# The last 16 up chunks of a transformer kernel by Strassen's method, with their weight sums made by adding DMAs from GpSimd's queue

## The chip, the core and the metric

One core of one Trainium2 chip. Engines: TensorE (PE), VectorE (DVE), ScalarE (ACT), GpSimd (POOL), SyncE (SP), 16 DMA engines. The metric is the device time of one execution in microseconds (us); the kernel before takes 1288.5 us in the median of three runs (1288.05 to 1291.14).

## The reference

Two transformer blocks over 512 tokens of 1024 features, all float32. The last part is the one that matters here:

```
def conv_ffn(xn, w_up, conv_w, conv_b, w_down):
    h = xn @ w_up                       # 1024 -> 2 x 2816
    a, b = jnp.split(h, 2, axis=-1)
    c = causal depthwise convolution of a, 3 taps, + conv_b
    return (jax.nn.gelu(c, approximate=False) * b) @ w_down

def second_block(...):
    z = rmsnorm(h, mix_norm_g) @ w_in
    ... pool, rwkv and differential attention mixers ...
    h = h + y @ w_out
    h = h + memory_cross_attention(...)
    h = h + conv_ffn(rmsnorm(h, ffn_norm_g), w_up, conv_w, conv_b, w_down)
```

The first block (two kinds of attention, gates, output projections) and the mixers of the second take the first 926 us of the span.

## The kernel before

**Arithmetic.** Every float32 factor is split into a high half (ACT copies it to the type float32r) and a low half (raw minus high, on DVE or POOL). A product is three matmuls: high x high, high x low, low x high (`mm3`, L488 is the matmul itself). Activations are laid out as [128 features, tokens], so the weights are the stationary operand and the tokens the moving one.

**The stream of weights.** SP loads 85 chunks of 1 MB (8 k x 256 columns for 128 partitions) into a ring of three raw slots (L2615; L2569 for the first 15). ACT makes the high half of a chunk (L1192) in a ring of two, as soon as the chunk before the last is used up; POOL makes the low half in four parts of 512 columns (`low_weights`, L2499), and PE waits part by part. Each engine works through its instructions in the order written; there is no planner.

**Up stage.** For each j of 11, two chunks (half a, half b), each with two tiles of 128 features: 4 x 8 x 3 = 96 matmuls of 512 columns. The four results go to banks 0 to 3 in turn. DVE moves an `a` tile out of its bank times the inverse norm (L2411), does the three taps (L2413 to L2415), ACT does the gelu (L1818), DVE multiplies with the norm and with the `b` tile in its bank (L2433, L2435). The forms for the down stage are made tile by tile (L2421, L2424, L2425, high half L1211, low half L1855).

**Down stage.** It already works by Strassen's method in the Winograd form: 2x2 quarters of the weights and of the activations, seven products with 4 pieces of weights each, DOWN = 28 pieces, each 11 k x 3 matmuls of 256 columns (the token half). A piece has its own bank; DVE adds it to `xres` (L2441), and some products start on the bank of an earlier one once that has been moved. Pieces are loaded by SP (L2631, 704 KB), high half on ACT (L1202), low half on DVE (L1855) or, for the first four and each fourth, on POOL (L2557).

**Sums of the down weights.** Four of the seven products need sums of quarters of the weights (S1 to S4). They are made in DRAM (`sums_kept`) in the first 460 us: ACT issues plain copies of a quarter (S1 and S3 from A21 at L1367, S2 from S1 at L1392, S4 from S2 at L1496), and POOL adds another quarter by adding DMAs, four per sum (`add`, L2509), which stand in its queue between the low halves of chunks 15 and 16, 17 and 18, 22 and 23, 34 and 35. POOL waits for the copy before it issues the adds.

## Time and profile before

| | |
|---|---|
| median of 3 runs | 1288.5 us |
| profiled execution | 1291.47 us, its span 1289.7 us |
| mean granted TensorE clock | 0.997 |
| PE / DVE / ACT / POOL busy | 97 / 54 / 44 / 41% |
| up stage, first matmul to first matmul of down | 926.27 to 1174.53 us |
| down stage, to its last matmul | 1286.51 us |

The span is the time from the first to the last instruction in the profile; the execution's own time is a little longer. A busy share is the time in which an engine had at least one instruction in work. Matmuls overlap: one of 512 columns is recorded with some 396 ns, but they start every 234 ns, so the pace is read from starts, not from lengths.

### The profile page before, as it was taken

The numbers are of one execution on the slowest core, as the hardware profiler recorded it, in microseconds if no ns is written. First come the engines' busy times: TensorE is split into PE (matmuls) and PEld (weight loads), VectorE is DVE, ScalarE is ACT, GpSimd is POOL, SyncE is SP. The second block draws the span as 40 slices with busy tenths as digits, with TensorE's granted clock in tenths as the row PEclk, the third lists the DMA queues.
The fourth block names the chain that finished last, engine by engine and source line by source line (L and its number), as shares of the span: only waits on it lengthen the run. The fifth ranks groups of instructions, "written<-read, shape, count | busy, mean of one in ns | idle before, by whom it ended". The sixth has DMA issues, their size and how long they took to land.

```text
span 1289.7 us, 20794 instructions
## 1 busy us (share of the span) xinstructions
PE 1253.3 (97%) x8570; PEld 1019.5 (79%) x8570; DVE 699.2 (54%) x1093; ACT 568.5 (44%) x870; POOL 530.7 (41%) x424
## 2 busy tenths in 40 slices
PE   6999999999999999999998899999999999999999
PEld 5788888866678888767786767788788888888999
DVE  3250004886431266686557657265565665766773
ACT  6541444786665233354544544353422221224452
POOL 6544454322234544534242126331444444546321
PEclk9999999999999999999999999999999999999999
DMA  9836795612115452412220013310222222224554
GB/s 387 348 131 243 248 230 191 163 50 97 51 66 188 122 163 79 181 66 76 69 107 16 3 66 131 135 61 34 99 98 98 81 87 94 99 88 172 166 185 151
DMA packets 24907, 165.05 MB, mean 128 GB/s; under 512 B 2792, under 2 KB 2920, under 8 KB 11504
## 3 DMA queue, kind: packets, MB, share of 16 engines
q1 hardware_dynamic: 20448, 128.15, 27.9%
q10 hardware_dynamic: 2064, 24.07, 5.0%
q0 software_dynamic: 2304, 11.54, 4.5%
q8 instruction: 68, 1.11, 0.3%
q14 instruction: 23, 0.19, 0.0%
HBM read 157.43 MB, written 29.38 MB: 145 GB/s over the span
## 4 chain that ended last, share of the span: by engine, by line
PE 89%; DVE 4%; ACT 3%; POOL 2%; issue 1%; DMA 0%; SPq 0%; DVEq 0%; ACTq 0%
PE banks L488 87%; PE banks L495 2%; DVE arena L1985 1%; POOL h_low L2557 1%; DVE arena L1982 1%; DVE arena L1987 1%; POOL weights_low L2557 1%; DMA arena<-in_mem 0%; ACT weights_high L1192 0%; ACT arena L1238 0%; ACT memory_high L1248 0%; ACT arena L1416 0%; ACT arena L1417 0%; ACT arena L1415 0%; DVE arena L1943 0%
## 5 line engine op out<-in xcount | busy, mean ns | idle before, releaser
L2499 POOL TENSOR_TENSOR weights_low<-weights,weights_high 128x512 fp32r<-128x512 f32 x324 | 433.2, 1367 | 580.5 <-ACT weights_high L1192 580.5
L488 PE MATMUL banks<-h_high_low,weights_high 128*128 128x512 f32 x880 | 358.2, 407 | 1.6 <-ACT arena L1443 1.6
L488 PE MATMUL banks<-h_low,weights_high 128*128 128x512 f32 x880 | 348.9, 397 | 0.0
L488 PE MATMUL banks<-h_high_low,weights_low 128*128 128x512 f32 x880 | 348.8, 396 | 0.0
L1192 ACT ACTIVATE weights_high<-weights 128x2048 fp32r<-128x2048 f32 (+2 forms) x90 | 156.3, 1737 | 243.1 <-PE banks L488 226.0
L488 PEld LDWEIGHTS banks<-h_high_low,weights_high 128*128 128x128 f32 x880 | 166.0, 189 | 46.0 <-issue 5.8
L488 PEld LDWEIGHTS banks<-h_low,weights_high 128*128 128x128 f32 x880 | 166.0, 189 | 41.8 <-issue 3.6
L488 PEld LDWEIGHTS banks<-h_high_low,weights_low 128*128 128x128 f32 x880 | 165.8, 188 | 40.4
L488 PE MATMUL banks<-arena 64*64 64x64 f32 (+6 forms) x1800 | 118.1, 263 | 4.1 <-issue 2.6
L488 PEld LDWEIGHTS banks<-arena 64*64 64x64 f32 (+3 forms) x1800 | 85.9, 148 | 29.9 <-issue 23.2
L1238 ACT ACTIVATE arena<-banks 128x256 f32<-128x256 f32 (+4 forms) x82 | 41.9, 519 | 53.4 <-PE banks L495 35.1
L2411 DVE TENSOR_TENSOR arena<-banks,sums 128x512 f32<-128x512 f32 x22 | 15.2, 692 | 78.1 <-PE banks L488 73.0
L488 PE MATMUL banks<-t_high,weights_low 128*128 128x256 f32 x198 | 55.6, 281 | 0.0
L488 PE MATMUL banks<-weights_high,h_high_low 128*128 128x256 f32 (+1 forms) x192 | 55.3, 288 | 0.3 <-ACT arena L1238 0.3
L488 PE MATMUL banks<-weights_high,h_low 128*128 128x256 f32 (+1 forms) x192 | 54.2, 282 | 0.0
L488 PE MATMUL banks<-weights_low,h_high_low 128*128 128x256 f32 (+1 forms) x192 | 54.1, 282 | 0.0
L1221 ACT ACTIVATE sums<-xres 128x512 f32<-128x512 f32 x32 | 20.2, 631 | 70.3 <-DVE xres L2065 39.3
L1938 DVE COPY arena<-banks 128x256 f32<-128x256 f32 (+3 forms) x40 | 25.3, 632 | 47.1 <-PE banks L488 46.2
L488 PE MATMUL banks<-t_high,weights_high 128*128 128x256 f32 x154 | 43.5, 283 | 2.5 <-issue 1.5
L488 PE MATMUL banks<-t_high,h_high_low 128*128 128x256 f32 x154 | 42.7, 277 | 0.0
L2557 POOL TENSOR_TENSOR weights_low<-weights,weights_high 128x384 fp32r<-128x384 f32 (+1 forms) x20 | 21.3, 1094 | 47.3 <-ACT weights_high L1202 47.3
L495 PE MATMUL banks<-consts,arena 128*128 128x128 f32 x245 | 37.2, 277 | 1.6 <-DVE arena L2222 0.8
(360 smaller groups left out, 2371.9 us busy)
## 6 DMA issues: line engine op xcount, KB each, us to landing
weights<-in_stream SPq DMA_DIRECT2D x82, 1024.0 KB, 4.8
sums_kept<-in_down POOLq DMA_DIRECT2D x16, 704.0 KB, 12.8
arena<-in_ada SPq DMA_DIRECT2D x8, 1024.0 KB, 11.9
weights<-in_down SPq DMA_DIRECT2D x9, 704.0 KB, 4.1
weights<-sums_kept SPq DMA_DIRECT2D x9, 704.0 KB, 4.0
sums_kept<-in_down ACTq DMA_DIRECT2D x2, 2816.0 KB, 21.4
sums_kept<-sums_kept ACTq DMA_DIRECT2D x2, 2816.0 KB, 12.6
h<-sums_kept SPq DMA_DIRECT2D x7, 704.0 KB, 4.2
```

What stands on the lines that cost most here:

```text
L488: ins = nc.tensor.matmul(o, lhsT, rhs, start=start, stop=stop, skip_group_check=skip)
L495: ins = nc.tensor.transpose(o, i, ident[0:rows, 0:rows])
L1192: nc.scalar.activation(hi_of(c)[:, cols], raw_of(c)[:, cols], ACT.Copy)\
L1221: nc.scalar.activation(SQ[n][i % 2][:, 0:width], src[:, k, 0:width], ACT.Square)\
L1238: nc.scalar.activation(dst, s_, ACT.Copy).then_inc(ring_.out(key), 1)
L1938: nc.vector.tensor_copy(dst, o if src is None else src(o)).then_inc(ring_.out(key), 1)
L1982: link(stt(w, o[:, :, 0:end], 0.0, w, ALU.max, ALU.add))
L1985: ins = nc.vector.tensor_tensor_scan(v, ones(end), v, 0.0, ALU.mult, ALU.add)
L1987: tt(w, o[:, :, 0:end], w, ALU.subtract).then_inc(M2.out(("a", i)), 1)
L2411: tt(a[:, 2:T + 2], o, rms[:, :], ALU.mult).then_inc(M.out(("up", m, 0)), 1)
L2499: nc.gpsimd.tensor_tensor(lo_of(c)[:, cols], raw_of(c)[:, cols], hi_of(c)[:, cols].bitcast(F32), ALU.subtract).then_inc(sem("weights_split ...
L2557: nc.gpsimd.tensor_tensor(down_lo(i)[:, cols], down_raw(i)[:, cols], down_hi(i)[:, cols].bitcast(F32), ALU.subtract).then_inc(sem("down_lo ...
```

## The change

- The up stage does only 3 of its 11 j in the old way (`UP_PLAIN`), six chunks, with banks 0 to 5 in turn. `STREAM` is 69 in place of 85.
- The other 16 tiles of `a` and 16 of `b` are 16 Strassen chunks (`UP`). Each is a 2x2 scheme: the 1024 inputs (k) in two halves, two tiles of 128 outputs, the 512 tokens in two halves; even chunks are two tiles of `a`, odd chunks the two tiles of `b` beside them. A chunk has seven products (P1, R5, P3, P6, R7, Q4, P2) of 4 k x 3 matmuls of 256 columns. The order is in `UP_STEPS`: in step i products P1 and R5 of chunk i, Q4 and P3 of chunk i-1, R7, P6 and P2 of chunk i; the last chunk has another order. In a chunk P6 adds onto the bank of P1, Q4 onto R7's, P3 onto R5's, each after what is there has been copied or moved.
- Weights come as 112 pieces of 256 KB, two by two (pairs): six raw slots, four high slots, cut out of the old rings. ACT makes the high half of a pair (1024 columns), DVE the low half, for 2 of 7 pairs POOL (2 x 512 columns).
- ACT copies P1 and P6 (`keep`), DVE makes the four quarters of a chunk in five moves (`up_out`), ACT does the first tap and its bias (`tap`), DVE the other two. The norm is multiplied into the tokens beforehand (`h_raw`), so the moves of the Strassen chunks have no multiplication by it. The token sums (4) and seven low and high halves are made during the plain chunks.
- The forms of the down stage are made in another order, mostly at the start of the product before; only each fourth piece's low half is on POOL.
- All sums of weights, for down and now for up (`up_sums`, 4 sums of 4 MB), are made from POOL's queue: 8 plain copies and 32 adding DMAs. ACT issues none. SP waits for all of them before the first up piece.

The core of the diff:

```diff
-STREAM = 85
+UP_PLAIN = 3
+UP = 2 * (KF // 2 - UP_PLAIN)
+STREAM = 63 + 2 * UP_PLAIN
+KH, TH = KD // 2, T // 2
+UP_STEPS = [[(c, f) for c, fs in ((i, (P1, R5)), (i - 1, (Q4, P3)), (i, (R7, P6, P2))) if 0 <= c < UP for f in fs]
+            for i in range(UP + 1)]
+UP_STEPS[UP - 1] = [(c, f) for c, fs in ((UP - 1, (P1, R5, R7, P6)), (UP - 2, (Q4, P3)), (UP - 1, (P2,))) for f in fs]
+PAIR_RAW, PAIR_HI = 6, 4
+PAIRS_POOL = [q for q in range(UP_PAIRS) if q % 7 in (2, 5)]
...
-        FROM_POOL = tuple(i for i in range(DOWN) if i < DOWN_PAIRS or i % DOWN_PAIRS == 0)
+        DOWN_FREE = [104, 108, UP_N, UP_N, UP_N]
+        FROM_POOL = tuple(i for i in range(DOWN) if i % DOWN_PAIRS == 0)
... PE
-            for j in range(KF // 2):
+            M.use([0, 1, 2, 3, 4, 5])
+            for j in range(UP_PLAIN):
...
+            for n, (c, f) in enumerate(UP_SEQ):
+                if f == P6:
+                    pe.wait_ge(sem("up_copied"), 2 * c + 1)
+                elif f == Q4:
+                    pe.wait_ge(sem("product_moved"), moved_at(c, SUM3))
+                elif f == P3:
+                    pe.wait_ge(sem("product_moved"), moved_at(c, C22))
+                elif c < 2:
+                    M.take(pe, ("up", c, f, "bank"))
+                elif f == P1:
+                    pe.wait_ge(sem("up_copied"), 2 * (c - 2) + 2)
+                else:
+                    pe.wait_ge(sem("product_moved"), moved_at(c - 2, {R5: C12, R7: C21, P2: C11}[f]))
+                q = n // 2
+                if q in PAIRS_POOL:
+                    pe.wait_ge(sem("piece_low_pool"), 2 * PAIRS_POOL.index(q) + n % 2 + 1)
+                elif n % 2 == 0:
+                    pe.wait_ge(sem("piece_low"), PAIRS_DVE.index(q) + 1)
+                if c == 0:
+                    pe.wait_ge(sem("token_split"), T_ORDER.index(f) + 1)
+                for k in range(KH):
+                    mm(o, whi[:, k, :], right[0], k == 0 and f not in (P6, Q4, P3), False, skip=True)
+                    mm(o, whi[:, k, :], right[1], False, False, skip=True)
+                    mm(o, wlo[:, k, :], right[0], False, last, sem("product_done") if last else None, skip=True)
... ACT
-            for to in (S1, S3):
-                act.dma_start(sums_kept[to], down_in[A21]).then_inc(sem("sums_copied"), 16)
+            for i, step in enumerate(UP_STEPS):
+                for c, f in step:
+                    if n and UP_SEQ[n - 1][1] in (P1, P6):
+                        keep(*UP_SEQ[n - 1])
+                    if n % 2 == 0:
+                        pair_high(n // 2 + 3)
+                    ... taps, gelus, first high halves
... DVE
+                if f == P2:
+                    moved_(tt(to_tile(c, 0, 0), up_bank(c, P2), k1, ALU.add))
+                    dve.wait_ge(sem("up_copied"), 2 * c + 2)
+                    moved_(tt(k3, up_bank(c, R7), k2, ALU.subtract))
+                    dve.wait_ge(sem("product_moved"), moved_at(c, SUM3))
+                    moved_(tt(to_tile(c, 1, 1), k3, up_bank(c, R5), ALU.subtract))
+                elif f == Q4:
+                    moved_(tt(to_tile(c, 1, 0), up_bank(c, Q4), k2, ALU.subtract))
+                else:
+                    moved_(tt(to_tile(c, 0, 1), up_bank(c, P3), k2, ALU.add))
+            for i, step in enumerate(UP_STEPS):
+                for c, f in step:
+                    if n:
+                        up_out(n - 1)
+                    if n % 2 == 1:
+                        low_pair((n + 5) // 2)
+                    if i % 2 == 1:
+                        ... first_form at R5, conv of one tile at P6
+                    elif i:
+                        if f == (R5 if i < UP else Q4):
+                            conv(up_tile(i - 2, 1), False)
+                        if f == P6:
+                            gact_out(i - 1)
... POOL
+            low_weights(0, 12)
+            copy(sums_kept[S1], down_in[A21])
+            copy(sums_kept[S3], down_in[A21])
+            low_weights(12, 15)
+            add_down(S1, A22, 2)
+            add_down(S3, A11, 2)
+            low_weights(15, 18)
+            copy(sums_kept[S2], sums_kept[S1], 2)
+            copy(up_sums[S1], up_in[A21])
+            low_weights(18, 20)
+            copy(up_sums[S3], up_in[A21])
+            low_weights(20, 22)
+            add_down(S2, A11, 5)
+            add_up(S1, A22, 5)
+            low_weights(22, 24)
+            add_up(S3, A11, 5)
+            low_weights(24, 26)
+            copy(sums_kept[S4], sums_kept[S2], 5)
+            copy(up_sums[S2], up_sums[S1], 5)
+            low_weights(26, 28)
+            add_down(S4, A12, 7)
+            add_up(S2, A11, 7)
+            low_weights(28, 33)
+            copy(up_sums[S4], up_sums[S2], 7)
+            low_weights(33, 36)
+            add_up(S4, A12, 8)
... SP
+            sp.wait_ge(sem("sums_added"), 8 * 16 * DOWN_PAIRS)
+            for n, (c, f) in enumerate(UP_SEQ):
+                    if q < PAIR_RAW:
+                        sp.wait_ge(used[last % RAW], last // RAW + 1)
+                    else:
+                        sp.wait_ge(sem("product_done"), 2 * (q - PAIR_RAW) + 2)
+                sp.dma_start(piece_of(pair_raw, n), up_from[f][c]).then_inc(pair_loaded(q)[0], 16)
```

The third argument of `copy` is the number of sums (four adds each) that must have landed, that of `add_down` and `add_up` the number of copies.

## Rows read from the trace of the kernel before

**Rows 1.** the page, parts 1 and 2: TensorE, its clock in 40 slices

```profile
PE 1253.3 (97%) x8570; PEld 1019.5 (79%) x8570; DVE 699.2 (54%) x1093; ACT 568.5 (44%) x870; POOL 530.7 (41%) x424
...
PEclk9999999999999999999999999999999999999999
```

**Rows 2.** chain of waits in order of time: start us, us, what

```profile
878.97 295.74 PE banks L488 x1274
...
1184.26 12.15 POOL h_low L2557 x8
```

**Rows 3.** timeline of PE (start us, us, engine, line, op): stage starts, last matmul

```profile
926.27 0.39 PE L488 MATMUL banks<-h_high_low,weights_high 128*128 128x512 f32 x1
...
1174.53 0.28 PE L488 MATMUL banks<-t_high,weights_high 128*128 128x256 f32 x1
...
1286.51 0.28 PE L488 MATMUL banks<-t_high,weights_low 128*128 128x256 f32 x1
```

**Rows 4.** timeline of POOL in the up stage, chunks two apart

```profile
951.89 5.05 POOL L2499 TENSOR_TENSOR weights_low<-weights,weights_high 128x512 fp32r<-128x512 f32 x4 [4.84 <-ACT weights_high L1192]
...
974.39 5.03 POOL L2499 TENSOR_TENSOR weights_low<-weights,weights_high 128x512 fp32r<-128x512 f32 x4 [5.39 <-ACT weights_high L1192]
```

**Rows 5.** timeline of DVE: its first move of the up stage, its last moves

```profile
935.40 0.69 DVE L2411 TENSOR_TENSOR arena<-banks,sums 128x512 f32<-128x512 f32 x1 [5.11 <-POOL arena L2550]
...
1279.04 0.42 DVE L2441 TENSOR_TENSOR xres<-xres,banks 128x256 f32<-128x256 f32 x1 [3.25 <-PE banks L488]
...
1286.82 0.42 DVE L2441 TENSOR_TENSOR xres<-xres,banks 128x256 f32<-128x256 f32 x1 [3.47 <-PE banks L488]
```

**Rows 6.** timeline of weight loads (PEld) at the start of the down stage

```profile
1191.74 0.19 PEld L488 LDWEIGHTS banks<-t_high,weights_high 128*128 128x128 f32 x1 [1.66 <-issue]
...
1195.04 0.19 PEld L488 LDWEIGHTS banks<-t_high,weights_high 128*128 128x128 f32 x1 [1.10 <-POOL h_low L2557]
```

**Rows 7.** groups by form, 870 to 1170 us: shapes, count, busy us, mean ns

```profile
L2499 POOL TENSOR_TENSOR weights_low<-weights,weights_high 128x512 fp32r<-128x512 f32 x96 | 130.5, 1389 | 165.1 <-ACT weights_high L1192 165.1
...
L2415 DVE SCALAR_TENSOR_TENSOR arena<-arena,params 128x512 f32<-128x512 f32 x22 | 26.3, 1194 | 0.8
...
L2421 DVE TENSOR_TENSOR arena<-arena 128x256 f32<-128x256 f32 x11 | 16.6, 1512 | 0.0
...
L1192 ACT ACTIVATE weights_high<-weights 128x2048 fp32r<-128x2048 f32 x24 | 46.0, 1915 | 155.3 <-PE banks L488 155.3
...
L1818 ACT ACTIVATE arena<-arena 128x512 f32<-128x512 f32 x22 | 13.6, 624 | 9.0 <-DVE arena L2415 9.0
```

**Rows 8.** three lines by themselves: ns of one, min/median/max, first and last start

```profile
L2415 DVE SCALAR_TENSOR_TENSOR arena<-arena,params x22: 752/754/1823, 937.5 to 1165.7; 128x512 f32<-128x512 f32 x22
...
L2425 DVE SCALAR_TENSOR_TENSOR arena<-arena x11: 411/420/1512, 1081.7 to 1178.6; 128x256 f32<-128x256 f32 x11
...
L1855 DVE TENSOR_TENSOR weights_low<-weights,h_high_low x8: 1619/1626/2170, 1189.2 to 1273.8; 128x1408 fp32r<-128x1408 f32 x8
```

**Rows 9.** DMA view, issues: count, KB each, median us to landing

```profile
sums_kept<-in_down POOLq DMA_DIRECT2D x16, 704.0 KB, 12.8
...
weights<-in_down SPq DMA_DIRECT2D x9, 704.0 KB, 4.1
...
sums_kept<-sums_kept ACTq DMA_DIRECT2D x2, 2816.0 KB, 12.6
...
out<-xres SPq DMA_DIRECT2D x8, 256.0 KB, 2.7
```

**Rows 10.** timeline of POOL: four adding DMAs, low halves of chunk 18

```profile
156.52 3.49 POOL L2509 DMA_DIRECT2D sums_kept<-in_down  x4
...
181.56 5.04 POOL L2499 TENSOR_TENSOR weights_low<-weights,weights_high 128x512 fp32r<-128x512 f32 x4 [1.36 <-ACT weights_high L1192]
```

**Rows 11.** line L2615 by itself: its 69 loads, us to landing

```profile
DMA to landing us min/median/max: 4.6/4.8/17.4
```

**Rows 12.** timeline of ACT: the chunk load that it waits for

```profile
149.08 1.91 ACT L1192 ACTIVATE weights_high<-weights 128x2048 fp32r<-128x2048 f32 x1 [5.82 <-DMA weights<-in_stream]
```

More of the change, by code:

```diff
@@ L443, in down_loaded @@
             if s < RAW:
-                return loaded[s], 16 * ((STREAM + i % DOWN_RAW - 2) // RAW + 1 + turn)
+                return loaded[s], 16 * (sum(c % RAW == s for c in range(2, STREAM)) + turn + 1)
             return sem(f"first{s - RAW}_loaded"), 16 * (turn + 2)
@@ L1819, in _, with gelu, first_high_of @@
-            assert chunks[0] == STREAM + HI
-            for i in range(HI, DOWN):
+            def gelu(m):
+                act.wait_ge(sem("conv"), m + 1)
+                nc.scalar.activation(gact_raw[:, m, :], gact_raw[:, m, :], ACT.Gelu).then_inc(sem("gelu"), 1)
+            def first_high_of(m):
+                if m < DOWN_K:
+                    if m < 2 * UP_PLAIN:
+                        M.wait_out(act, ("up", m, 1))
+                    else:
+                        act.wait_ge(sem("forms_made"), made_at("gact", m))
+                    high(t_hi[0][:, m, :], q11[:, m, :], sem("forms_hi"))
@@ new lines, in _ @@
+            split_weights()
+            for m in range(2):
+                gelu(m)
+            split_weights()
+            for i, f in enumerate(T_ORDER):
+                act.wait_ge(sem("token_made"), KD + 4)
+                high(th_hi[f], th_raw[f], sem("token_hi"))
+            split_weights()
+            for m in range(2):
+                first_high_of(m)
+            for m in range(2, 4):
+                gelu(m)
+            split_weights()
+            for m in range(2, 4):
+                first_high_of(m)
@@ new lines, in _, with form_high @@
+            for _ in range(HI):
+                split_weights()
+            assert chunks[0] == STREAM + HI
+            def form_high(f):
+                act.wait_ge(sem("product_done"), UP_N + DOWN_PAIRS * (f - 1))
+                for g, (first, last) in enumerate(GROUPS):
+                    act.wait_ge(sem("forms_made"), {R5: made_at("T1", DOWN_K - 1), P6: made_at("T2", g), R7: made_at("T3", g),
+                                                    Q4: made_at("T4", g)}.get(f, made_at("gact", KF - 1)))
+                    high(t_hi[f % 2][:, first:last, :], form_raw[f][:, first:last, :], sem("forms_hi"))
@@ L1821, in _ @@
+            down_high(1)
+            form_high(R5)
+            for i in range(2, DOWN):
                 down_high(i)
@@ new lines, in gact_out @@
+            def gact_out(c):
+                for half in range(2):
+                    m = up_tile(c, half)
+                    dve.wait_ge(sem("gelu"), m + 1)
+                    if half == 0:
+                        dve.wait_ge(sem("product_moved"), moved_at(c, C12))
+                    tt(gact_raw[:, m, :], gact_raw[:, m, :], other[:, half, :], ALU.mult).then_inc(sem("forms_made"), 1)
+                    if m >= DOWN_K:
+                        first_form(m)
+            for m in range(2):
+                conv(m, True)
@@ new lines, in add_up @@
+            def add_up(to, what, copied):
+                pool.wait_ge(sem("sums_copied"), 16 * copied)
+                for p in range(DOWN_PAIRS):
+                    chunks = slice(UP // 4 * p, UP // 4 * (p + 1))
+                    pool.dma_start(up_sums[to, chunks], up_in[what, chunks], accum_op=ALU.add, max_dma_last_dim=8192)\
+                        .then_inc(sem("sums_added"), 16)
+            low_weights(0, 12)
+            copy(sums_kept[S1], down_in[A21])
+            copy(sums_kept[S3], down_in[A21])
```

422 lines of the change are left out of this document (282 added, 140 removed).

## The prediction

> **What bounds the kernel now.** I read the page first: PE is busy for 97% of the span, and the granted clock is in the top tenth in all 40 slices [rows 1], so TensorE runs at its 2.4 GHz level and the clock is no term. The chain of waits in order of time says the same for the part that changes: from 878.97 us on it is matmuls, except for a hop over ACT and POOL up to 1196 [rows 2]. A busy PE can still wait inside, so next come single matmuls. The up stage starts at 926.27, the down stage at 1174.53, the last matmul at 1286.51 [rows 3]. In the up stage POOL's work on one weight chunk (48 matmuls of 512 columns) recurs every 22.50 / 2 = 11.25 us [rows 4], so 22 chunks take 247.5 of the 248.26 us between the two starts; the rest (0.8 us) is the norm's matmul. The up stage has no waits: it is bound by matmuls alone. In the down stage the last products end 3.89 us apart (7.78 / 2) for 33 matmuls of 256 columns [rows 5], 0.1179 us each; 28 products need 108.9 us and take 112.1, so 3.2 us are waits, 2.8 of them seen as two idle gaps of weight loads at 1191.7 and 1195.0 [rows 6], where POOL's and DVE's low halves came late.
>
> **The matmuls.** Of 22 plain chunks 6 stay; 16 go: 16 x 11.25 = 180.0 us out. In comes Strassen's method: 16 chunks x 7 products x 4 k x 3 = 1344 matmuls of 256 columns. The up stage of before has none of these, but the down stage has the same form (fp32r parts, 128x128 weights, 256 columns) at 0.1179 us: 158.5 us in. Net -21.5 us. The ends of that price: half of a 512-column matmul (0.2344 / 2 = 0.1172) gives 157.5, and 0.12 gives 161.3; it is a small uncertainty. The shorter products (12 matmuls against 33) bring a wait every 1.41 us, but in the down stage products with a wait at each k run at the same pace.
> The Trainium skill, page "TensorE: Matmul & The Clock Gate", section "Back-to-back issue gap", speaks against the change: it gives a sustained 131 ns at 512 columns and 81 ns at 128; read linearly (an estimate from that page, 98 ns at 256), 768 large ones would be 101 us, 1344 small ones 132 us, and the change would cost 31 us. The trace decides otherwise: 234 and 118 ns, a ratio of 1.99.
>
> **DVE in the Strassen part**, by two chunks (14 products, 168 matmuls, 19.8 us). An op with two SBUF inputs and 256 columns takes 0.41 to 0.42 alone, one of 1408 takes 1.62 [rows 8], so 1.04 ns a column, and 1024 columns 1.22. Five of the seven weight pairs get their low half here: 6.1. Ten moves of products: 4.2. Four taps of the convolution at 0.75 (752 to 754 ns undisturbed [rows 8]; L2415's mean of 1194 has POOL beside it [rows 7]): 3.0. Two products with the gelu at 0.69: 1.4. Forms for the down stage: 0.8 to 1.7. Sum 15.5 to 16.4. While POOL subtracts, DVE's two-input ops stretch: L2421 takes 1.51 where 0.42 is its length alone, and so loses 1.1; L2415 loses 0.44 on average [rows 7, 8]. Over the 96 POOL ops of that stretch these two groups alone lose 11 x 1.1 + 22 x 0.44 = 21.8, so a POOL op costs DVE at least 0.23 and at most 1.1; I take 0.6. There are 4 POOL ops in 19.8 us, so +2.4 (0.9 to 4.4). DVE needs 18 to 19 of 19.8 us: under PE, but near.
> ACT: seven high halves of 1024 columns (between 0.62 at 512 and 1.92 at 2048 [rows 7]: 1.05) 7.4, two taps, two gelus, four copies of products and up to two forms at 0.62 at most: 6.2; 13.6 of 19.8. POOL 4 x 1.39 = 5.6.
> The order matters as much as the sums. The tightest handover is product Q4 of the chunk before: it adds onto the bank of R7, and waits for DVE's SUM3, which waits for P2. Two products of the next chunk lie between (P1, R5: 2.8 us); DVE needs 2 moves, 0.84. So it may come 2 us late to P2. From P3 to P2 it has 4.2 us and, in even steps, one move, two low halves at most, the gelu products and forms, some 4.5 to 5.3: it is late by 0.3 to 1.1 there, and is not seen by PE. A low half is ordered five products (7.1 us) ahead of its use. I put 1.5 us on this (0 to 8, below).
>
> **The start of it.** DVE begins at 935.40 [rows 5]; the plain chunks end at 926.27 + 0.8 + 67.5 = 994.6. In between, DVE does 6 convolutions (2.84 each, 17.0), 8 scalings of the tokens (6.0), 4 sums (4.9), 7 low halves of the sums (8.5), 5 gelu products (6.9), 4 forms (1.7) and 2 low pairs (2.4): 47.4 of 59.2 us, with 16 POOL ops at 0.6 another 9.6, and 2.3 us of waiting for the second product: 59.3. The last piece is fixed: product (5, up) is full at 983.3, after it DVE has 2.84 + 0.8 + 2.4 + 1.4 = 7.5 us, to 990.8, if it is punctual, and the bank of tile 4 is wanted at 994.6. Six banks for the plain chunks keep the sums of tokens between a product and its move from stopping PE: the fifth tile needs the bank of a gelu product that DVE gives back by about 960, wanted at 971. I take 1.0 us (0 to 4).
>
> **The down stage** keeps its 924 matmuls. The 3.2 us of waits had their cause in four low halves on POOL at the start; now POOL has one of four. But DVE has new ops in the first two forms: 6 to 7 low halves, 7 groups of forms, about 18 us of work in the first 15.6 us, and the third piece's weights are loaded only when the last up product is done. That load (4.1 us [rows 9]), its high half behind four form halves on ACT (6.0) and its low half (1.6) end at about 7.7, wanted at 7.8. I take 1.5 us of waits in place of 3.2: -1.7 (-3.2 to +1).
>
> **The sums of weights.** POOL's queue gets 8 plain copies (4 of them ACT's before) and 32 adding DMAs instead of 16: 24 issues more. Four adds took 3.49 us of POOL's queue [rows 10], 0.87 each: 21 us of POOL time, spread over 103 to 460 us, where POOL works 5 of 11.25 us. What is queued behind a wait on POOL are the low halves of the next chunk, and behind these PE. The nearest: after chunk 17 (at 177) POOL waits until two groups of four adds, issued from 139, have landed, before it issues two copies. A group takes 20 us (landing 12.8 us in the median, the last 20.1 [rows 9]), so they land at 179 to 181; low halves of chunk 18 ran at 181.56 [rows 10] and PE wants them at 187.8. Next, after chunk 21 (220.6) it waits for five copies: 11.2 MB at 2.8 MB in 12.6 us [rows 9] from 181 on, to about 231, and issues eight adds until 238; chunk 22 ran at 235.6 and is wanted some 15 us later. After 305 the gaps are longer. Loads of chunks share the DMA engines: the slowest of before took 17.4 us [rows 11], and ACT waited 5.8 us for it [rows 12] with no wait of PE behind. The copies that disturbed it now run 17 us earlier. I take 0.5 us (0 to 5, and the rivals). ACT is rid of 4 issues of 0.5 to 1.1 us in a stretch that it partly bounds: at most -1, taken as 0.
>
> **Sum.** -21.5 + 1.5 + 1.0 - 1.7 + 0.5 = -20.2. The profiled execution spans 1289.7 us and took 1291.47; the sum makes the span 1269.5. The runs' median is 1288.5, 3 us under the profiled one; moved by the same amount: 1268.3 us. With no wait anywhere it is 1288.5 - 21.5 - 3.2 = 1263.8.
>
> **Rivals.** (B) DVE becomes the bound of the Strassen part. For: at 1.1 us per POOL op it needs 20.8 us per 19.8, and its queue has three waits on products in each step, at which a late start isn't made up. Against: the taps went to ACT and the multiply by the norm is gone. Price: 1 to 2 us x 8 pairs of chunks, with a late start: +8 to +16, 1276 to 1284, say 1280.
> (C) POOL's queue holds PE in the first 460 us. A wait costs PE what it lasts beyond 187.8 - 1.3 - 139 = 47.5 us for both groups of adds (40 in my sum). Up to 60 us gives +12, 1280; from 69 us on, 1.7 times the time of before, PE loses more than 21 us in this place alone and the kernel is slower: at twice the time (80), +32, 1301. For: adds and copies now overlap, and eight adds stand in line. Against: in the trace no group exceeded 20 us beside chunk loads. The Trainium skill, page "SBUF — State Buffer", section "A bandwidth-pool intuition that's wrong", warns that DVE's two-port modes keep GpSimd from writing descriptors (a DMA of 620 ns becomes 3100); by it 24 issues could cost 60 us of POOL. The trace shows 3.3 to 3.5 us for four issues each time.
> (D) The pieces are 256 KB in rows of 2 KB, loaded every 1.41 us, 185 GB/s. The nearest row is the output, 256 KB in 2.7 us [rows 9]; the room is 4 products, 5.7 us. If short rows allow only 150 GB/s, the 28.7 MB take 191 us: +33, 1301. From 160 GB/s down the kernel is slower.
> (E) The change does what it says and gains under 0.3%: it needs B and C together; 1287.
>
> **How the numbers follow.** Mine 0.66 (1264 to 1273), B 0.16, C 0.12 (0.05 of it slower), D 0.03, E 0.03. The range 1263 to 1283 takes in B and the mild part of C and leaves out 0.15. A measurement tells 0.3% (3.9 us) from no change. Faster 0.89, same 0.03, slower 0.08.
>
> **What would show it.** Right: the distance from the first up matmul to the first of down is near 229 us, P2's products recur every 9.9 us, weight loads have gaps of 1 us or so at the start of both Strassen parts. PE waiting for DVE's moves at Q4 is B; PE waiting for L2499 before 460 us is C; ACT waiting for DMA in the pair's high halves is D. The prediction is wrong if a matmul of the new part takes more than 0.12 us, or if PE waits more than 5 us in any of the stages.

## The result, and the profile after

| | before | after |
|---|---|---|
| median (lowest to highest), 20 runs each | 1289.1 us (1286.9 to 1291.1) | 1291.3 us (1288.7 to 1295.6) |
| profiled execution's span | 1289.7 us | 1290.6 us |
| mean granted clock | 0.997 | 0.991 |

The ratio after/before is 1.0018 (95% interval 1.0010 to 1.0026): no change by the bound of 0.3%, though the interval puts after a little behind (2.2 us in the medians), where 1268.3 us was forecast. The two profiled executions lie above their medians, that of before by 2.4 us and that of after by 1.2, so their spans differ by only 0.9 us. 16 chunks of matmuls became cheaper as predicted, and four waits of PE, with a lower clock behind each, took all of it back. The page after, first lines and clock [rows 1]:

```profile
PE 1238.9 (96%) x9146; PEld 1039.3 (81%) x9146; DVE 754.7 (58%) x1166; ACT 623.3 (48%) x958; POOL 511.5 (40%) x404
...
PEclk9999998999999999999999999999999899999999
```

The clock is no longer in the top tenth everywhere: a digit 8 stands in the slice from 194 us and in that from 1000 us. PE's timeline has the stage starts that answer to [rows 3], and between them the three long waits (in brackets: idle time before the instruction, and what released it):

```profile
210.58 0.77 PE L576 MATMUL banks<-h_high_low,weights_high 128*128 128x512 f32 x1 [6.45 <-POOL weights_low L2789]
...
934.22 0.40 PE L576 MATMUL banks<-ffn_high,weights_high 128*128 128x512 f32 x1
...
1008.13 0.58 PE L576 MATMUL banks<-h_high_low,weights_high 128*128 128x256 f32 x1 [5.67 <-DVE arena L2610]
...
1170.23 0.58 PE L576 MATMUL banks<-token_sum_high,weights_high 128*128 128x256 f32 x1 [3.35 <-DVE sums L2650]
...
1174.62 0.28 PE L576 MATMUL banks<-t_high,weights_high 128*128 128x256 f32 x1
...
1287.48 0.28 PE L576 MATMUL banks<-t_high,weights_low 128*128 128x256 f32 x1
```

So the up stage starts 7.95 us late (934.22 against 926.27); the plain chunks, 68.3 us of work, take 73.9; the Strassen part takes 166.5 instead of 158.5; the down stage takes 112.9 where it took 112.0. Together 7.95 + 5.6 + 8.0 + 0.9 = 22.4 against the 21.5 won. Compared matmul by matmul, PE is 2.2 us behind the kernel before from 125 us on (chunk 12), 10.5 us behind from 210.58 us on, and regains 2.6 us between 600 and 755 us. (That last part differs by some us between executions of all the kernels here.)

**Wait 1, early.** ACT's timeline shows the wait for a chunk load that answers to [rows 12]; the line of the loads by itself gives the landing times that answer to [rows 11]; the third row is the DMA view of 181.6 to 207.2 us, the life of that load:

```profile
207.19 1.91 ACT L1310 ACTIVATE weights_high<-weights 128x2048 fp32r<-128x2048 f32 x1 [14.10 <-DMA weights<-in_stream]
...
DMA to landing us min/median/max: 4.6/4.8/25.5
...
q0 software_dynamic: 147, 6.49, 72.0%
q1 hardware_dynamic: 266, 1.97, 22.4%
```

In that window POOL's queue (q0) moved 6.49 MB in 147 packets, 44 KB each; the chunk loads (q1) 1.97 MB in 266, 7.4 KB each. The copies of sums ran beside the loads of two chunks. PE then waits 6.45 us for POOL's low half (the first of the long waits above).

**Waits 2 and 3** are DVE's. Its timeline, ahead of the start and in the last chunk, with the one line of POOL's that lies beside the first two:

```profile
975.99 2.33 DVE L2041 TENSOR_TENSOR h_low<-h,h_high_low 128x1024 fp32r<-128x1024 f32 x1
978.24 2.31 DVE L2041 TENSOR_TENSOR token_sum_low<-arena,token_sum_high 128x1024 fp32r<-128x1024 f32 x1
...
975.47 17.43 POOL L2789 TENSOR_TENSOR weights_low<-weights,weights_high 128x512 fp32r<-128x512 f32 x8 [7.50 <-ACT weights_high L1310]
...
1005.60 1.75 DVE L2608 TENSOR_TENSOR arena<-arena,sums 128x512 f32<-128x512 f32 x1
1007.38 0.69 DVE L2610 TENSOR_TENSOR arena<-banks,arena 128x512 f32<-128x512 f32 x1
...
1166.81 1.30 DVE L2602 SCALAR_TENSOR_TENSOR arena<-arena,params 128x512 f32<-128x512 f32 x1 [0.89 <-ACT arena L1938]
1168.15 1.36 DVE L2603 SCALAR_TENSOR_TENSOR arena<-arena,params 128x512 f32<-128x512 f32 x1
1169.44 0.41 DVE L2648 TENSOR_TENSOR forget_rows<-banks,sums 128x256 f32<-128x256 f32 x1
1169.77 0.41 DVE L2650 TENSOR_TENSOR sums<-banks,sums 128x256 f32<-128x256 f32 x1
```

Seven token low halves of 2.31 us each (two of them are shown), beside eight operations of POOL that take 2.2 us each instead of 1.39, stand ahead of gact of tile 4 (L2608, L2610), which frees the bank that the first Strassen product wants. In the last chunk the two taps of the conv of the tile before (L2602, L2603) stand ahead of C11 and SUM3 (L2648, L2650), for which Q4 waits.

**The clock behind a wait.** Seven windows of after; the last three numbers are the granted clock, the DMA share and GB/s, and the x behind PE's time counts its matmuls:

```profile
1005.00:1010.00 5.00, 1.87 (x8) 1.87 (x9) 4.93 (x6) 1.13 (x2) 3.22 (x2) 0.62 0.08 10
1010.00:1015.00 5.00, 5.00 (x32) 5.00 (x32) 1.28 (x2) 1.45 (x2) 0.00 (x0) 0.70 0.70 218
...
1015.00:1160.00 145.00, 145.00 (x1227) 145.00 (x1226) 116.57 (x170) 82.39 (x116) 46.54 (x30) 1.00 0.56 183
...
1160.00:1165.00 5.00, 5.00 (x44) 5.00 (x44) 1.38 (x2) 1.25 (x2) 0.00 (x0) 1.00 0.29 115
...
1170.00:1175.00 5.00, 4.77 (x28) 4.77 (x29) 2.62 (x6) 0.93 (x3) 0.10 (x1) 0.66 0.00 0
...
1195.00:1200.00 5.00, 4.03 (x24) 4.06 (x25) 5.00 (x8) 2.47 (x3) 1.52 (x1) 0.74 0.38 137
...
200.00:300.00 100.00, 93.05 (x631) 72.28 (x630) 70.03 (x85) 65.19 (x91) 43.39 (x37) 0.97 0.91 238
```

Undisturbed, a window of 5 us counts 44 matmuls (1160 to 1165 us), at the 2.4 GHz level (clock 1.00); 0.62 and 0.70 mean that part of the window ran at the 1.2 GHz level. Behind the 5.67 us wait the first 100 matmuls of the Strassen part take 14.13 us from start to start; in e7_three below, where the clock doesn't fall there, they take 12.00. So 2.1 us are lost, 0.4 of the wait again. Behind the 3.35 us wait the 24 matmuls up to the down stage take 4.39 us, and 2.96 in e6_fill, whose clock stays at 1.00 there: 1.4 us. Behind a wait of 2.03 us at 1195.97 some 1.4 us are lost: with the same wait and no fall of the clock, the down stage of e1_small is that much shorter. From 200 to 300 us the clock is 0.97, where the kernel before has 1.00; PE falls 8.4 us behind there, 6.45 of wait and so 1.9 of clock. The third row is the long undisturbed stretch: no wait of PE, 1227 matmuls in 145 us, DVE busy for 80%.

The loss behind a wait isn't a constant. The same 24 matmuls behind the same wait (3.35 to 3.38 us) in after, e1_small and e6_fill:

```profile
1170.23:1174.62 4.39, 4.39 (x24) 4.39 (x25) 2.24 (x4) 0.63 (x1) 0.00 (x0) 0.63 0.00 0
```

```profile
1161.87:1167.16 5.29, 5.29 (x25) 5.29 (x26) 2.24 (x4) 0.63 (x1) 0.00 (x0) 0.50 0.00 0
```

```profile
1169.13:1172.09 2.96, 2.96 (x25) 2.96 (x26) 2.15 (x4) 0.63 (x1) 0.00 (x0) 1.00 0.00 0
```

So 1.4, 2.3 and 0 us. Nothing in the three kernels differs at that place.

### The profile page after: what moved, and what is told of

It is laid out like the page before. It is cut to its first block, busy times and chain, and to the rows that moved or that the text cites. A ratio compares the mean times of both kernels' runs of the same rounds, so it can differ in the third digit from the quotient of the medians.

```text
span 1290.6 us, 22227 instructions
## 1 busy us (share of the span) xinstructions
PE 1238.9 (96%) x9146; PEld 1039.3 (81%) x9146; DVE 754.7 (58%) x1166; ACT 623.3 (48%) x958; POOL 511.5 (40%) x404
## 4 chain that ended last, share of the span: by engine, by line
PE 80%; DVE 9%; DMA 4%; ACT 4%; issue 2%; POOL 1%; SPq 0%; DVEq 0%; ACTq 0%
PE banks L576 78%; DMA weights<-in_stream 2%; PE banks L583 2%; DMA weights<-in_with_f 1%; DVE arena L2171 1%; ACT weights_high L1310 1%; DVE arena L2173 1%; DVE arena L2168 1%; DVE h L2672 1%; DVE h_low L2041 1%; DVE token_sum_low L2041 1%; DVE arena L2608 1%; POOL weights_low L2789 0%; DMA h<-in_down 0%; DVE arena L2602 0%
## 5 line engine op out<-in xcount | busy, mean ns | idle before, releaser
L2789 POOL TENSOR_TENSOR weights_low<-weights,weights_high 128x512 fp32r<-128x512 f32 (+1 forms) x260 | 355.6, 1403 | 476.1 <-ACT weights_high L1310 476.1
L576 PE MATMUL banks<-h_high_low,weights_high 128*128 128x512 f32 (+1 forms) x784 | 291.4, 372 | 13.7 <-POOL weights_low L2789 6.4
L576 PE MATMUL banks<-h_low,weights_high 128*128 128x512 f32 (+1 forms) x784 | 282.4, 360 | 0.0
L576 PE MATMUL banks<-h_high_low,weights_low 128*128 128x512 f32 (+1 forms) x784 | 282.0, 360 | 0.0
L576 PEld LDWEIGHTS banks<-h_low,weights_high 128*128 128x128 f32 x784 | 149.0, 190 | 25.5 <-issue 3.4
L576 PEld LDWEIGHTS banks<-arena 64*64 64x64 f32 (+3 forms) x1800 | 85.2, 147 | 28.7 <-issue 22.0
L2878 POOL TENSOR_TENSOR weights_low<-weights,weights_high 128x512 fp32r<-128x512 f32 x32 | 49.8, 1576 | 116.8 <-ACT weights_high L1322 116.8
L1322 ACT ACTIVATE weights_high<-weights 128x1024 fp32r<-128x1024 f32 x56 | 58.9, 1057 | 36.1 <-PE banks L576 36.1
L2041 DVE TENSOR_TENSOR weights_low<-weights,weights_high 128x1024 fp32r<-128x1024 f32 (+1 forms) x45 | 57.0, 1268 | 17.8 <-ACT weights_high L1322 13.7
L576 PE MATMUL banks<-token_sum_high,weights_high 128*128 128x256 f32 x192 | 55.1, 287 | 3.3 <-DVE sums L2650 3.3
L576 PE MATMUL banks<-token_sum_high,weights_low 128*128 128x256 f32 x192 | 55.2, 287 | 0.0
L576 PE MATMUL banks<-token_sum_low,weights_high 128*128 128x256 f32 x192 | 55.1, 287 | 0.0
```

The costliest lines, as they stand in the source:

```text
L576: ins = nc.tensor.matmul(o, lhsT, rhs, start=start, stop=stop, skip_group_check=skip)
L1322: nc.scalar.activation(pair_hi(q), pair_raw(q), ACT.Copy).then_inc(sem("piece_hi"), 1)
L2041: return tt(lo, raw, hi.bitcast(F32), ALU.subtract).then_inc(done, 1)
L2789: nc.gpsimd.tensor_tensor(lo_of(c)[:, cols], raw_of(c)[:, cols], hi_of(c)[:, cols].bitcast(F32), ALU.subtract).then_inc(sem("weights_split ...
L2878: nc.gpsimd.tensor_tensor(piece_of(pair_lo, n), piece_of(pair_raw, n), piece_of(pair_hi, n).bitcast(F32), ALU.subtract).then_inc(sem("piec ...
```

## The experiments

Each ran in five rounds beside runs of the kernel before; "ratio" is to that kernel. Edits are to the changed kernel unless said otherwise. Where the text says that a run is some us faster than after, it subtracts medians; the runs were not taken beside after, and the kernel before moved between 1288.9 and 1290.0 us from group to group, so such a difference is good to about 1 us.

| run | median us | ratio (95%) |
|---|---|---|
| e1_small | 1282.0 | 0.9937 (0.9919 to 0.9955) |
| e2_nosum | 1282.3 | 0.9945 (0.9927 to 0.9963) |
| e3_last | 1289.6 | 1.0000 (0.9989 to 1.0012) |
| e4_start | 1284.1 | 0.9955 (0.9938 to 0.9972) |
| e5_std | 1287.3 | 0.9977 (0.9964 to 0.9989) |
| e6_fill | 1289.7 | 0.9997 (0.9987 to 1.0007) |
| e7_three | 1273.1 | 0.9869 (0.9855 to 0.9884) |
| e8_four | 1274.0 | 0.9878 (0.9863 to 0.9892) |
| e9_pool | 1270.7 | 0.9853 (0.9837 to 0.9868) |
| e10_best | 1270.3 | 0.9840 (0.9827 to 0.9853) |
| e11_before_small | 1289.3 | 0.9994 (0.9982 to 1.0006) |
| e12_four | 1286.6 | 0.9982 (0.9965 to 0.9998) |
| e13_rotate | 1287.6 | 0.9985 (0.9973 to 0.9997) |
| e14_best | 1267.8 | 0.9833 (0.9815 to 0.9851) |
| e15_rot_only | 1270.8 | 0.9858 (0.9836 to 0.9880) |

### The early part: rows of the copies

```diff
-pool.dma_start(to, what).then_inc(...)
+pool.dma_start(to, what, max_dma_last_dim=8192).then_inc(...)
```

> The change with one edit: the eight plain copies of weight sums go out in rows of at most 8 KB, as the chunk loads have them, where they now have some 44 KB. Theory (a chunk load's 7.4 KB packets stand behind the copies' large ones on each DMA engine): the load of chunk 12 lands in about 10 us, not 17.7, that of chunk 19 in 5 to 10 us, not 25.5; PE's stalls of 3.5 and 6.4 us there go, the up stage starts near 926 us, and the time is 1283 to 1286 us. Rival 1 (the amount moved counts, not the size of a packet): loads and stalls as they are, 1291 us. Rival 2 (more descriptors keep POOL longer at each issue and make low halves late): issues of 2 us and more each, 1291 us or above.

Measured 9.3 us less, more than expected. The loads' landing times, the wait of ACT and the window of 200 to 300 us in this run:

```profile
DMA to landing us min/median/max: 4.6/4.8/12.5
...
202.63 1.92 ACT L1310 ACTIVATE weights_high<-weights 128x2048 fp32r<-128x2048 f32 x1 [7.41 <-DMA weights<-in_stream]
...
200.00:300.00 100.00, 99.15 (x685) 76.78 (x684) 73.02 (x89) 66.90 (x93) 39.51 (x34) 1.00 0.90 240
```

The worst load takes 12.5 us, not 25.5, though the same copies go over the same queue; PE doesn't wait, the clock of 200 to 300 us is 1.00 again and the up stage starts at 924.98. The size of the rows was the cause. Rival 1 is out, and so is rival 2: POOL's issues of copies take 0.62 to 0.64 us each in e1_small, 0.52 to 0.55 in after. What large rows would have cost from ACT's queue, at the same times, was not run.

The next run leaves all up sums out:

```diff
-up_from = [up_in[A11], up_sums[S1], up_sums[S4], up_sums[S2], up_sums[S3], ...]
+up_from = [up_in[A11], up_in[A21], up_in[A12], up_in[A21], up_in[A11], ...]
```

> The change without any sum of up weights (4 copies and 16 adding DMAs gone; the pieces that would be sums are plain quarters, so that part of the weights is another than it should be); the down sums stay as they are. Theory (the copies delay chunk loads): chunk 19, beside which two up copies run, loads in under 8 us and PE's stall of 6.4 us goes; chunk 12, beside which only down copies run, still takes some 17 us and keeps its 3.5 us. Time 1283 to 1285 us. Rival (the offset of the early part comes from elsewhere, such as low halves behind issues in POOL's queue): offset stays above 8 us, time 1289 to 1291.

A little faster than expected, and within 0.3 us of e1_small: with small rows the up sums (four copies of 4 MB, 16 adding DMAs of 1 MB) cost nothing that can be measured. The 3.5 us at chunk 12 did not stay, though: its load landed in 12.8 us here, in 10.7 and 13.3 us in the next two runs and in 17.7 in the profile of after. PE's delay around chunks 12 and 13 changes from execution to execution (0.4 to 2.3 us wherever the copies have large rows, none in e1_small); the wait for the second chunk (4.9 to 6.5 us) is in the profile of every run that has the up sums and large rows.

The control is the kernel before with the same edit:

> The kernel before with only the rows of its four plain copies (on ACT's queue) cut to 8 KB. Theory (what the small rows won in the changed kernel, 9.3 us, was a new loss of the change, from copies that now fall beside the loads of chunks 12 and 19): before has little of it, 0 to 2 us, 1287.5 to 1289.5. Rival (large rows cost the kernel before as much, and the change is credited with what any kernel could have): 1280 to 1284 us.

Nothing (0.9994). Its worst load went from 17.4 us [rows 11] to 12.4; ACT had waited for it, PE had not. So the 9.3 us are a loss that the change brought, not a gain that was open to any kernel.

### The last chunk

```diff
+def last_sums():            # SUM3 and C22 of chunk 15
+    ...
 up_out(n - 1)
+if (c, f) == (UP - 1, P2):
+    last_sums()
 ...
 if f == P6: conv(up_tile(i - 1, 0), False)
```

> The change with DVE's order of the last up chunk mended: SUM3 and C22 of it are made while its P2 is running, ahead of the conv of the tile before. Theory: PE's wait of 3.3 us ahead of Q4 goes, and with it the matmuls lost to the lower clock at 1170 to 1175 (some 1 us). What is late next is DVE's share of the down start, which waits 2.2 us at 1196 already: it gives back up to 3 us. Time 1287.5 to 1290. Rival (DVE is full from 1165 to 1200, so that all comes back there): 1291, with PE's wait at the second form of down 3 us longer.

```diff
-UP_STEPS[UP - 1] = [(c, f) for c, fs in ((UP - 1, (P1, R5, R7, P6)), (UP - 2, (Q4, P3)), (UP - 1, (P2,))) for f in fs]
```

> The change with one part undone: the last up chunk in the order that all other chunks have (P1, R5, Q4 and P3 of the chunk before, R7, P6, P2). Q4 of it stands directly behind its P2 either way; what differs is that the conv of the tile before then stands three products earlier in DVE's queue. Theory (the 3.3 us are the conv of 2.7 us ahead of SUM3, which the special order puts there): PE's wait ahead of Q4 falls to 1 to 1.5 us, for C11 and SUM3, the down stage starts 2 to 3 us earlier and gives 1 to 2 us of it back, as the run with the mended DVE order did: 1288 to 1290.5 us. Rival (the wait comes from having no product between P2 and Q4, in any order): 3 us stay, 1291 us.

PE's timeline of e3_last has no wait at Q4, but this one in the down stage; e5_std has the wait at Q4, but short:

```profile
1175.08 0.36 PE L578 MATMUL banks<-t_high,weights_high 128*128 128x256 f32 x1 [1.61 <-DVE weights_low L2043]
```

```profile
1167.92 0.39 PE L575 MATMUL banks<-token_sum_high,weights_high 128*128 128x256 f32 x1 [0.85 <-DVE sums L2649]
```

Both put the conv behind the sums or well ahead of them; the Strassen part takes 162.8 and 163.5 us instead of 166.5. e3_last gives 2.5 of its 3.7 us back in the down stage, as expected (115.3 us instead of 112.9). In e5_std nothing is given back (112.9 us there), though 1 to 2 us were expected. The special order gained nothing: undone, the kernel is 4 us faster in the median and its Strassen part 3.0 us shorter in the profile (2.5 of wait, and no fall of the clock behind the short one, against a slower pace of all its matmuls).

### The start

```diff
-for i, f in enumerate(T_ORDER): ... low(th_lo[f], ...)      # seven
+for i in range(5): token_low(i)
 ...
+if n in (2, 3): token_low(n + 3)
```

> The change with the last two of the seven token low halves (Q4, P3) made in the Strassen part, after the third and fourth product, instead of ahead of it. Theory (DVE's chain sets the start; a low half takes 2.31 us beside POOL): the first Strassen matmul comes 4 to 4.6 us earlier (1003.5 to 1004), its wait falls from 5.7 us to about 1, and the clock that is lost behind it (0.62 and 0.70 at 1005 to 1015, some 2 us of matmuls) with it: 1284.5 to 1287.5 us. Rival (ACT's gelu at 1001.7 or the bank is what comes last, or the two low halves hold the moves of chunk 0 up): 1290 to 1291.

7.2 us less; the wait is 0.85 us, and the windows 1005 to 1010 and 1010 to 1015 count 44 matmuls each at clock 1.00. How much of this was clock is for the next run:

```diff
+pe.wait_ge(sem("token_split"), 1)
+for i in range(20):
+    mm(bank[7][...], th_hi[P1][:, 0, 0:P], th_hi[P1][:, 0:2, :], ...)
 M.use([4, 5, 6, 7, 0, 1, 2, 3])
```

> The change with 20 more matmuls of 512 columns (4.7 us of work, into a bank that is overwritten later, nothing else uses them) in PE's queue where it waits 5.67 us for the start of the Strassen part. Theory (the matmuls missing in 1005 to 1015 are lost to the clock that falls because PE stood still): the first Strassen matmul comes when it did, the granted clock stays near 1.00 behind it, where it was 0.62 and 0.70, and the down stage starts 2 to 2.5 us earlier: 1288.5 to 1289.5 us. Rival (the slow matmuls are slow for another reason, such as operands or banks): clock and pace stay, 1291 us or, with the extra work, more.

The windows of 1005 to 1015 us in e6_fill:

```profile
1005.00:1010.00 5.00, 3.86 (x23) 3.00 (x23) 4.93 (x6) 1.26 (x2) 3.25 (x2) 1.00 0.33 120
1010.00:1015.00 5.00, 5.00 (x44) 5.00 (x44) 1.90 (x2) 1.89 (x4) 0.00 (x0) 1.00 0.37 108
```

The start is where it was (1007.92), the clock stays at 1.00, and the first 100 matmuls take 12.27 us instead of 14.13: 1.9 of the 2.1 us are back. That the missing matmuls are lost to the clock, and the clock to PE's standing still, is shown in the profile; in the median (1.6 us less) it is at the edge of what can be told. That the whole Strassen part is 2.3 us shorter (164.2 instead of 166.5) agrees only by chance. Here the clock didn't fall behind the wait at Q4 (1.4 us less), and the 1100 matmuls in between took 131.12 us instead of 130.24 (0.9 more, see the last section).

Then one that went against my theory, six banks undone:

```diff
-M.use([0, 1, 2, 3, 4, 5])
+M.use([0, 1, 2, 3])
```

> The change with one part undone: the six plain up chunks take four banks in turn, as in the kernel before, not six. DVE's sums and low halves of the tokens (some 25 us) then stand ahead of the move that frees a bank. Theory: the b tiles of the third j wait up to 7 us for tiles 2 and 3 to be multiplied, which stand behind the seven token low halves, and the start of the Strassen part comes that much later: 1295 to 1299 us. Rival (the banks come free in time, since two chunks are 22 us of matmuls): 1291 us.

Forecast 4 to 8 us slower, measured 4.7 faster (12 runs from 1281.4 to 1292.9). PE waits 2.22 us at 989.97 for a bank, as the theory has it (7 were expected), but not at the Strassen start. The cause is which bank is used, not how many: with six in turn, tile 4's product with the gelu lies in bank 4, and that is the bank of the first Strassen product. The test with the same chain of DVE:

```diff
-M.use([0, 1, 2, 3, 4, 5])
+M.use([4, 5, 0, 1, 2, 3])
```

> The change with the six banks of the plain chunks taken in the order 4, 5, 0, 1, 2, 3, not 0 to 5: the last two tiles then lie in banks 2 and 3, and bank 4, which the first Strassen product takes, is freed some 20 us before. DVE's chain is as long as before. Theory (the wait of 5.67 us is for bank 4): the Strassen part follows the plain chunks within 0.5 us, no clock is lost at 1005 to 1015, the time is 5 to 7.5 us lower, 1284 to 1286 us. Rival (DVE's chain is late for everything, so the next thing that it makes, the low half of the next pair, is late next): at most 2 us, 1289 us or more.

```profile
1004.95 0.36 PE L576 MATMUL banks<-h_high_low,weights_high 128*128 128x256 f32 x1 [2.17 <-issue]
```

In between (1287.6 us, 1284 to 1286 by the theory and 1289 or more by the rival), 3.8 us less than after. The wait falls from 5.67 to 2.17 us with no clock lost behind it, and PE no longer waits for a bank at the start; but DVE's low halves of the first pairs (L2041, 2.36 us for two from 1003.62 on, so the first is done near 1004.9) are the next thing that is late. That last step is read from the times; the profile names no releaser. So 3.5 us were the bank, 2.2 the length of the chain.

### Combinations, and the down stage

> Small packets of the copies, the two late token low halves and the mended DVE order of the last chunk together. If the three are independent: 1291.3 less 9.3, 7.2 and 1.7, so 1273 us. If the later ones only give time to waits that come behind: 1276 and more. The earlier start of down should show DVE as what PE waits for at 1155 to 1185, some 4 to 5 us in all.

The three gains add up: 18.2 us of the 18.2 expected, to within the 1 us or so of such differences. The down stage shows DVE as what PE waits for, three times, 4.4 us in all. The Strassen part takes 159.3 us.

```diff
 if f == P3:
+    stt(rows(q11), rows(q22), -1.0, rows(q11), ...)      # T2, from f == R5
     tt(rows(q12), rows(q12), rows(q22), ...)
```

> The three together, and the T2 sums (four of 1.76 us on DVE) moved out of the first four pieces of the down stage into the next four. Theory (DVE is full from 1165 to 1200, and second_low comes 2.2 us late behind T2): the waits for second_low go, 2 to 3.5 us faster than the three alone, 1270 to 1271 us. Rival (DVE is short over all eight pieces, so what leaves the first four is missing in the second four): within 1 us of the three alone, with PE's waits at the third form in place of those at the second.

The rival was right in time (0.9878 against 0.9869, no difference), and in place: the waits for second_low are gone, one of 2.49 us for the third form's halves has come. Next, two of GpSimd's low halves:

```diff
-FROM_POOL = tuple(i for i in range(DOWN) if i % DOWN_PAIRS == 0)
+FROM_POOL = tuple(i for i in range(DOWN) if i % DOWN_PAIRS == 0 and i not in (4, 8))
```

> The four edits together, and two pieces of the down stage (the fifth and the ninth) have their low half on DVE, not on GpSimd. Theory (beside GpSimd's work a DVE low half of 768 columns takes 1.44 to 1.77 us, alone 0.94, and there are four such operations of GpSimd to a piece: GpSimd's help costs DVE some 3 us and saves it 1.6): PE's wait of 2.5 us at the third form shrinks by 1 to 2 us, 1272 to 1273 us. Rival (the longer DVE operations are not GpSimd's doing): the wait grows by the 1.6 to 3.2 us of the two more low halves, 1275 to 1277 us.

A low half of DVE in e8_four, then in e9_pool:

```profile
1165.00 1.44 DVE L2043 TENSOR_TENSOR second_low<-arena,t_high 128x768 fp32r<-128x768 f32 x1
1168.73 1.48 DVE L2043 TENSOR_TENSOR second_low<-arena,t_high 128x768 fp32r<-128x768 f32 x1
```

```profile
1165.77 0.95 DVE L2043 TENSOR_TENSOR second_low<-arena,t_high 128x768 fp32r<-128x768 f32 x1
1168.51 0.95 DVE L2043 TENSOR_TENSOR second_low<-arena,t_high 128x768 fp32r<-128x768 f32 x1
```

With more to do, DVE is ahead: the wait shrinks from 2.49 to 1.15 us and the down stage from 113.8 to 112.1. Four runs a side put the medians 3.3 us apart, more than the 1 to 2 us expected and than the 1.7 seen in the profile. GpSimd's help cost more than it gave here.

```diff
+if i == UP and f == P3: down_high(1)
 if f == (Q4 if i < UP else P3): gelu(...)
```

> The same, and ACT makes the high half of the second down piece ahead of the last gelu but one of the up stage. PE waits 1.56 us for that piece's low half; ACT could start it 1.3 us earlier, so 1 to 1.3 us less than the run without it if DVE takes it up at once, nothing if DVE's move of the last product (0.4 us, just ahead of it) is what is late. 1271 to 1272.5 us.

> As the best version, but with the seven token low halves where the change has them, ahead of the start. Theory (bank 4 was all): within 1 us of the best version, 1269 to 1271 us. Rival (DVE's chain matters by itself): 1272 us or more, with PE waits in the first two Strassen chunks.

> The other rotation of banks together with all edits so far (small rows of the copies, two late token low halves, the mended last chunk, T2 later, two low halves of down from GpSimd to DVE, the high half of the second down piece earlier). If the edits at the start cure the same wait, only the 0.9 us that PE still waits there are left to win: 1269 to 1270 us.

The high half (e10_best) takes the wait at the second piece from 1.61 to 0.17 us, but the median falls by 0.3 us only, which can't be told from nothing. The rotation and the late low halves are not the same cure: with the rotation alone (e15_rot_only) PE still waits 2.18 us at the start, with both (e14_best) not at all. The medians (3 us apart, of four and five runs) can't confirm it, since the intervals overlap and 1270.8 us also lies in the range of the theory that bank 4 was all. The best version is 1.67% faster than the kernel before, 21.1 us. That its 1267.8 us lie beside the 1268.3 forecast for the change is no confirmation of the forecast: seven edits were needed for it, which the sum didn't have. Its stage starts:

```profile
924.11 0.40 PE L578 MATMUL banks<-ffn_high,weights_high 128*128 128x512 f32 x1
...
1152.37 0.28 PE L578 MATMUL banks<-t_high,weights_high 128*128 128x256 f32 x1
...
1263.15 0.28 PE L578 MATMUL banks<-t_high,weights_low 128*128 128x256 f32 x1
```

The up stage takes 228.26 us.

## Why the prediction was wrong, step by step

- **The matmuls (-21.5): right.** 0.1184 us each from start to start (130.24 us for 1100 of them) against 0.1179 in the sum, 0.7 us over all 1344; the pace per chunk is 9.95 us, and in the best version the two starts lie 228.3 us apart, 229 were forecast. The gap that spoke against the change (Trainium skill, "TensorE: Matmul & The Clock Gate", section "Back-to-back issue gap") is not seen here either: 0.118 us at 256 columns, 0.234 at 512.
- **DVE in the steady part: right in sign, too high in size.** 18 to 19 us of 19.8 were forecast, DVE is busy for 80% (15.9 us), and PE never waits there. Rivals B and D are out as they were put: DVE is not the bound of the steady part, and the 256 KB pieces land in 2.8 us. (D's own sum has a slip: 112 pieces of 262144 bytes are 29.4 MB, not 28.7.)
- **Handovers (+1.5, 0 to 8): failed in one place.** "Two products of the next chunk lie between" P2 and Q4 holds, or four lie there, for 15 chunks. In the last none lies there, and its order was in the diff; I did not walk through it. It cost 3.35 us and 1.4 of clock (2.3 in e1_small).
- **The start (+1.0, 0 to 4): failed.** 5.6 us, and 2.1 of clock. The right question was asked (when is tile 4 moved), with a wrong price and a bank overlooked. Seven low halves were 8.5 us by the length alone plus 0.6 for each op of POOL; they took 7 x 2.31 = 16.2 beside eight such ops, about 1 per op, close to my upper bound. The eight scalings (8.5 us for 6.0) and the four sums (8.0 for 4.9) ran beside POOL too. The sum of 59.3 in 59.2 us said that there was no slack at all, and I still took 1.0. And the bank that tile 4 frees is wanted by the first Strassen product: the condition "if it is punctual" carried everything.
- **The down stage (-1.7, -3.2 to +1): +0.9, in the range, but not the way that was forecast.** The load and the third piece were in time. DVE is busy for 19.65 of the 20 us from 1180 on, second_low came 2.0 us late, and the clock took 1.4. In e1_small and e4_start, with that wait and no fall of the clock, the stage takes 111.5 and 111.4 us, 0.5 less than before.
- **The sums (+0.5, 0 to 5): failed, 8 us, and this is the largest miss.** Of them 6.45 are one wait and 1.9 the clock behind it. Rival C looked at the right queue and the wrong resource: POOL's wait for its adds was 0.42 us, its issues of copies 0.5 to 0.7 us each; four adds of up weights at 233.50 us took 4.53 us instead of 3.49 [rows 10]. The warning in the Trainium skill's "SBUF — State Buffer", section "A bandwidth-pool intuition that's wrong", on descriptors held up by DVE, is not seen here at its price. It is hardly tested either: DVE did nothing from 178 to 200 us, where two of the copies were issued. What held PE was the load of a chunk behind large packets. The sign that I had given for C, PE waiting for POOL's low halves before 460 us, did appear and would have misled: POOL waited for ACT's high half, ACT for the load. I had the sentence on it ("copies that disturbed it now run 17 us earlier"), had [rows 11, 12] with 17.4 us of landing and 5.8 us of waiting, and did not ask how much of PE's slack was left when the load grows by another 8 us.
- **"The clock is no term": failed.** True of the kernel before, nearly: its profile has a mean of 0.997. Each new wait of 2 to 6.5 us cost 1.4 to 2.1 us more behind it in the profile of after; in all 2.1 + 1.4 + 1.4 + 1.9 = 6.8 us. No term of the sum held this.

Without the clock's share, 6.8 of the 22.4 us lost, a gain near 6 us would have been left. The terms that missed are independent, and I had added their middles as if one could not fail beside another.

## What to carry to other kernels

Price a wait of some microseconds that a change adds at its length and anything from nothing to 0.7 of it again (2.1 behind 5.67, 1.9 behind 6.45, 1.4 or nothing behind 2.03, and 0, 1.4 or 2.3 behind 3.35, by the execution), when the engine that waits is the one that the clock is granted to. Walk through the first and the last turn of a pipelined loop, with the bank or buffer of each product: the steady part was right at once, and all of PE's new waits in the up stage lay at its two ends. A bulk copy in the background is not free because its bytes fit: cut its rows to the size of the rows that the urgent loads use (8 KB here, the only size tried).

## What the runs showed of the hardware that was not expected

- DMA engines share by packet, as it looks: with 44 KB packets beside 7.4 KB ones a 1 MB load took 25.5 us (2 MB in 25.6 us for the whole queue); with rows of at most 8 KB on both sides the worst took 12.5 us, with the same copies. That the engines take turns packet by packet was not measured by itself.
- Behind a wait of PE of 3 to 6 us the 5 us windows show a granted clock of 0.62 to 0.70, and 20 further matmuls in the wait prevent it. It doesn't fall every time: in the kernel before 1.7 and 1.1 us [rows 6] cost nothing, the 3.38 us at the last chunk cost nothing in e6_fill, and behind the 2.03 us of the down stage it fell in after and e6_fill and not in e1_small and e4_start. What decides it no run here shows.
- The same clock makes part of the scatter. Two executions with the same early code (e10_best, e14_best) start the up stage at 929.67 and 924.11. Of the 5.6 us, 1.8 are there by 300 us, at clock 1.00 in both from 200 on; 1.6 come at 540 to 560 us, where the clock is 0.91 against 1.00; 1.7 come at 740 to 755, where it falls in both, in one for longer (0.54 and 0.78 in two windows of 5 us against 0.66 in one).
- The 1100 matmuls of 256 columns from the 100th to the 1200th of the Strassen part, without a wait, take 130.24 us in after, e7_three, e8_four, e10_best, e12_four, e13_rotate and e15_rot_only, and 131.12 in the eight others (0.1184 and 0.1192 us each), at a granted clock of 1.00 in both. Why there are two paces is open, and with one trace of each kernel it can't be told whether the kernel or the execution sets it.
- Beside subtractions on GpSimd a two-input op of DVE of 1024 columns takes 2.31 us, not 1.22, and one of 768 columns 1.44 to 1.48, not 0.95. GpSimd pays as well: its eight ops of 512 columns beside the seven low halves take 2.2 us each, 1.39 on average in the kernel before [rows 7].
